# Alternating two kinds of head pairs in an attention stage, with a one-operation difference of two softmaxes

## The chip, the cores and the metric

The kernel runs on one core of a Trainium2 chip. The metric is the device time of one launch in microseconds (us), lower is better. Everything is fp32; large matmuls are made of three passes over high and low parts. The whole program is two transformer blocks in one launch. Only one stage of some 120 us of it is touched: the first mixer of the second block.

## The reference, cut to what matters

The stage mixes two kinds of attention over 256 tokens (x) and 256 context tokens (ctx). Kind A is windowed attention with a sink, 8 heads of 64 that share 2 key-value heads. Kind B is differential attention, 4 heads with two score maps each:

```
def diff_attend(q, k, v, lam):
    s = jnp.einsum('bqhmd,bkhmd->bhmqk', q, k).astype(jnp.float32) * (HEAD_DIM ** -0.5)
    p = jax.nn.softmax(s, axis=-1)
    w = p[:, :, 0] - lam * p[:, :, 1]
    return jnp.einsum('bhqk,bkhe->bqhe', w.astype(v.dtype), v)
...
    y_b = sweep_blocks(lambda q_blk, n: diff_attend(q_blk, k_all, v_all, lam), bq, Q_BLOCK)
    y_b = rms_norm(y_b, b_sub_norm) * (1.0 - lam_init)
```

Query tiles of x see all 512 keys, those of ctx only the 256 context keys.

## The kernel before

The work is cut into 32 units, called pairs because each has two score maps: 4 query tiles of 128 rows (two of x, two of ctx), and in each tile 4 units B (one differential head) and then 4 units A (two windowed heads). `Attend` writes, for each engine, what step i of a software pipeline issues; every engine executes its own list in order, and semaphores join them.

- TensorE (PE), step i: the scores of unit i (L1792); then the transposes of the probabilities of unit i-2 (L1802), 4 blocks for B, 8 for A; then the product with the values of unit i-3 (L1814). The transposes of unit i-2 wait for its probabilities **and** for `aa_copied` of unit i-3, since both use the same psum banks.
- VectorE (DVE), step i: the maxima of unit i (B: L1870; A: L1874 and two L1878, with the bias); `weights` of unit i-1 (A: the reciprocal L1886; B: L1888 to L1891); for an A unit i-2 the copy of the second turned half (L1850); the output of unit i-3 (B: L1858, A: two L1860).
- ScalarE (ACT), step i: the two exponentials of unit i (L1827), then the copy of the turned probabilities of unit i-2 (L1836).

B's `weights` waited for by PE were four operations: reciprocal of both sums, times lambda, a scaling pass over map 1 (L1890), and a pass that scales map 0 and subtracts (L1891).

Beside these steps lie side steps, one behind an Attend step at most, whose places are (j, step) in the list `side`: the norms of the last context heads (L1648, L1660, L1663) and their turns (L1727 on PE, L1737 on ACT) in the first tile; then for each finished tile t the norm of B's outputs (`SubNorm`: the Square L1975 on ACT, L1986 to L1989 on DVE, Ln and Exp L1978, L1979 on ACT, L1992 and L1995 on DVE), and two output turns (L1727 on PE, L1737 on ACT for the high part, L1747 on DVE for the low part), one for B's columns (BQ) and one for A's (AQ). The next stage, the output projection with L350 and the weight splits L292 and L298, begins when the last output turn is done.

## Time and profile before

| | us |
|---|---|
| median of 3 runs | 2790.0 (2788.89 to 2799.0) |
| the profiled execution | 2799.45 |
| its span | 2797.7 |
| PE / DVE / ACT busy in the span | 2586.2 / 1378.7 / 1021.6 |
| the stage of the change, from the first scores to the first L350 of the next stage | 1301.2 to 1422.6 |

The span is the profiled part of the execution, 1.75 us shorter than its time. The profiled execution was slower than the median by 9.45 us, about as slow as the slowest of the three runs. The stage is 121.4 us, 4.3% of the span. On every timeline row the first number is the start from the span's start and the second the duration.

### The profile page before, as it was taken

What the parts mean: (1) busy time and instruction counts of PE and PEld (TensorE: products, weight loads), DVE (VectorE), ACT (ScalarE), POOL (GpSimd) and SP (SyncE); (2) the same over time, 40 slices, a digit from 0 to 9 for tenths busy, and PEclk for the clock granted to TensorE, in tenths of its full rate; (3) what the DMA queues carried; (4) which work ended last, traced back from release to release, by engine and by line L of the source; (5) the groups of instructions that cost most, each with busy time, mean ns of one, the idle gap of its engine ahead of it and who ended that gap; (6) DMA issues with size and microseconds to landing.
All of it is one profiled execution on the core that took longest, in us unless ns stands there. A gap on an engine that the chain in (4) does not pass through costs nothing. (4 is left out here: it accounts for less than half of the span.)

```text
span 2797.7 us, 36294 instructions
## 1 busy us (share of the span) xinstructions
PE 2586.2 (92%) x15294; PEld 2167.4 (77%) x15294; DVE 1378.7 (49%) x2279; ACT 1021.6 (37%) x1603; POOL 0.2 (0%) x4
## 2 busy tenths in 40 slices
PE   7999999899989999898888999989999896858999
PEld 6888689788868888776676888868888684546998
DVE  4646554654453333468754333343333535556654
ACT  4534444443342222255523222132222242244442
POOL 0000000000000000000000000000000000000000
PEclk8999999999999999999999999999999997679999
DMA  8886733688822223253012222222222352021454
GB/s 274 280 273 192 216 126 99 206 305 311 301 83 98 98 98 98 83 165 106 1 53 76 98 98 98 98 76 98 97 94 96 98 160 66 0 76 46 159 185 139
DMA packets 145188, 372.36 MB, mean 133 GB/s; under 512 B 20202, under 2 KB 65794, under 8 KB 144898
## 3 DMA queue, kind: packets, MB, share of 16 engines
q1 hardware_dynamic: 144594, 368.21, 40.0%
q8 instruction: 122, 2.00, 0.3%
q10 hardware_dynamic: 432, 1.82, 0.2%
q14 instruction: 40, 0.33, 0.0%
HBM read 368.84 MB, written 1.15 MB: 132 GB/s over the span
## 5 line engine op out<-in xcount | busy, mean ns | idle before, releaser
L298 DVE TENSOR_TENSOR weights_lo<-weights_raw,weights_hi 128x1024 fp32r<-128x1024 f32 (+1 forms) x545 | 656.3, 1216 | 536.5 <-ACT weights_hi L292 534.1
L350 PE MATMUL psum<-normed_hi,weights_hi 128*128 128x256 f32 (+1 forms) x2560 | 863.9, 337 | 33.0 <-DVE normed_lo L549 24.3
L350 PE MATMUL psum<-normed_lo,weights_hi 128*128 128x256 f32 (+1 forms) x2560 | 847.8, 331 | 0.0
L350 PE MATMUL psum<-normed_hi,weights_lo 128*128 128x256 f32 (+1 forms) x2560 | 847.3, 331 | 0.0
L292 ACT CAST weights_hi<-weights_raw 128x1024 fp32r<-128x1024 f32 (+1 forms) x545 | 562.2, 1039 | 378.7 <-DMA weights_raw<-in_w_down 265.1
L350 PEld LDWEIGHTS psum<-normed_hi,weights_hi 128*128 128x128 f32 x2560 | 489.1, 191 | 117.6 <-issue 51.4
L350 PEld LDWEIGHTS psum<-normed_lo,weights_hi 128*128 128x128 f32 x2560 | 490.5, 192 | 44.1 <-issue 1.2
L350 PEld LDWEIGHTS psum<-normed_hi,weights_lo 128*128 128x128 f32 x2560 | 490.0, 191 | 44.0
L350 PE MATMUL psum<-hidden_lo,weights_hi 128*128 128x512 f32 x528 | 205.4, 389 | 0.0
L350 PE MATMUL psum<-hidden_hi,weights_hi 128*128 128x512 f32 x528 | 205.4, 389 | 0.0
L350 PE MATMUL psum<-hidden_hi,weights_lo 128*128 128x512 f32 x528 | 205.4, 389 | 0.0
L452 DVE SCALAR_TENSOR_TENSOR resid<-psum,mod,resid 128x256 f32<-128x256 f32 x80 | 35.8, 480 | 273.3 <-PE psum L350 273.3
L350 PE MATMUL psum<-weights_hi,normed_hi 128*128 128x512 f32 (+2 forms) x400 | 151.0, 378 | 20.7 <-DVE weights_lo L298 10.8
L588 DVE TENSOR_TENSOR arena<-arena,psum 128x512 f32<-128x512 f32 (+1 forms) x110 | 63.9, 581 | 205.9 <-PE psum L350 205.9
L580 ACT CAST hidden_hi<-arena 128x512 fp32r<-128x512 f32 x66 | 40.9, 620 | 309.3 <-DVE arena L588 309.3
L350 PE MATMUL psum<-weights_hi,normed_lo 128*128 128x512 f32 (+2 forms) x400 | 147.8, 370 | 0.0
L350 PE MATMUL psum<-weights_lo,normed_hi 128*128 128x512 f32 (+2 forms) x400 | 147.7, 369 | 0.0
L577 ACT ACTIVATE arena<-psum 128x512 f32<-128x512 f32 (+1 forms) x110 | 56.3, 512 | 247.2 <-PE psum L350 247.1
L350 PEld LDWEIGHTS psum<-hidden_hi,weights_lo 128*128 128x128 f32 x528 | 99.1, 188 | 20.7
L350 PEld LDWEIGHTS psum<-hidden_hi,weights_hi 128*128 128x128 f32 x528 | 99.1, 188 | 20.6
L350 PEld LDWEIGHTS psum<-hidden_lo,weights_hi 128*128 128x128 f32 x528 | 99.1, 188 | 20.4
L350 PEld LDWEIGHTS psum<-weights_hi,normed_hi 128*128 128x128 f32 x400 | 82.1, 205 | 37.4 <-issue 12.9
(280 smaller groups left out, 2865.6 us busy)
## 6 DMA issues: line engine op xcount, KB each, us to landing
weights_raw<-in_w_gu SPq DMA_DIRECT2D x220, 512.0 KB, 3.5
weights_raw<-in_w_down SPq DMA_DIRECT2D x110, 512.0 KB, 3.5
arena<-in_w_mod SPq DMA_DIRECT2D x72, 512.0 KB, 6.4
weights_raw<-in_w_x SPq DMA_DIRECT2D x24, 512.0 KB, 4.7
resid<-in_w_mod SPq DMA_DIRECT2D x24, 512.0 KB, 6.3
normed_raw<-in_w_mod SPq DMA_DIRECT2D x24, 512.0 KB, 6.1
under_normed_hi<-in_w_mod SPq DMA_DIRECT2D x24, 512.0 KB, 6.3
weights_raw<-in_w_qk SPq DMA_DIRECT2D x24, 512.0 KB, 3.6
```

What stands on the lines that cost most here:

```text
L292: se.copy(w_hi[:, c % RING, a], w_raw[:, c % RING, a]).then_inc(hi_ready, 1)
L298: ve.tensor_tensor(w_lo[:, c % RING, a], w_raw[:, c % RING, a], w_hi[:, c % RING, a].bitcast(F32), ALU.subtract).then_inc(lo_ready, 1)
L350: last = te.matmul(out, a, b, start=start and n == 0, stop=stop and n == 2)
L452: last = ve.scalar_tensor_tensor(out=resid[:, k, mine], in0=psum[:, self.bank(k), side * S - at0:(side + 1) * S - at0], scalar=mod[:, m, s ...
L577: se.activation(raw, self.sums(b), ACT.Silu).then_inc(evac_act, 1)
L580: se.copy(hi, raw).then_inc(hid_hi, 1)
L588: ve.tensor_tensor(raw, raw, self.sums(b), ALU.mult).then_inc(evac_dve, 1)
```

## The change

Four edits, all in this stage. (1) The units of a tile alternate B, A, B, A instead of four B and four A. (2) `weights` of a B unit: lambda is kept negated, the factor -lambda * sum0 / sum1 is made in two small operations, and one long operation (map 1 times the factor plus map 0) gives the unscaled difference; the reciprocal of sum 0 is taken after it. (3) The output of a B unit is scaled as it leaves psum, a tensor_scalar in place of a copy. (4) SubNorm gets three more small operations for very small sums, and its steps and those of the output turns move: SubNorm from behind steps 8t+8 and 8t+9 to 8t+10 and 8t+11, the first output turn is now A's, the second B's.

```diff
@@ -1854,10 +1855,7 @@
                     at0 = 0
                     for n, dest in enumerate(u.out):
                         src = psum[:, 6, at0:at0 + dest.shape[1]]
-                        if u.lam is not None:
-                            last = ve.tensor_copy(dest, src)
-                        else:
-                            last = ve.tensor_scalar(dest, src, self.stat[:, j % 4, 2 + n:3 + n], None, ALU.mult)
+                        last = ve.tensor_scalar(dest, src, self.stat[:, j % 4, 2 + n:3 + n], None, ALU.mult)
                         at0 += dest.shape[1]
                     last.then_inc(aa_out, 1)
@@ -1885,12 +1883,12 @@
                 if u.lam is None:
                     step(ve.reciprocal(stat[:, 2:4], stat[:, 2:4]))
                     return
-                step(ve.reciprocal(stat[:, 2:4], stat[:, 2:4]))
-                step(ve.tensor_tensor(stat[:, 3:4], stat[:, 3:4], u.lam, ALU.mult))
-                step(ve.tensor_scalar(s[:, 1, 0:u.width], s[:, 1, 0:u.width], stat[:, 3:4], None, ALU.mult))
-                ve.scalar_tensor_tensor(out=s[:, 0, 0:u.width], in0=s[:, 0, 0:u.width], scalar=stat[:, 2:3],
-                                        in1=s[:, 1, 0:u.width], op0=ALU.mult, op1=ALU.subtract
-                                        ).then_inc(aa_probs, 1)
+                step(ve.reciprocal(stat[:, 3:4], stat[:, 3:4]))
+                step(ve.scalar_tensor_tensor(out=stat[:, 3:4], in0=stat[:, 3:4], scalar=stat[:, 2:3], in1=u.lam,
+                                             op0=ALU.mult, op1=ALU.mult))
+                ve.scalar_tensor_tensor(out=s[:, 0, 0:u.width], in0=s[:, 1, 0:u.width], scalar=stat[:, 3:4],
+                                        in1=s[:, 0, 0:u.width], op0=ALU.mult, op1=ALU.add).then_inc(aa_probs, 1)
+                step(ve.reciprocal(stat[:, 2:3], stat[:, 2:3]))
         BK, BV, AK, AV, BQ, AQ = 0, 512, 1024, 1152, 1280, 1792
         ab = at(0, TT, 2304)
@@ -1926,7 +1924,7 @@
                 ve.tensor_reduce(lam_tmp, lam_prod, AX.X, ALU.add).then_inc(lam_dots, 1)
                 dve.wait_ge(lam_ready, 1)
                 step(ve.tensor_tensor(lam, lam_tmp[:, 0:1], lam_tmp[:, 1:2], ALU.subtract))
-                step(ve.tensor_scalar(lam, lam, 0.8 - 0.6, None, ALU.add))
+                step(ve.tensor_scalar(lam, lam, -1.0, -(0.8 - 0.6), ALU.mult, ALU.add))
         def heads_of(a, t, start, heads):
             return a[:, t, start:start + heads * HD].rearrange("p (h d) -> p h d", d=HD)
@@ -1950,12 +1948,13 @@
                                      for side in range(2)],
                                     [ab[:, t, AQ + (4 * side + h) * HD:AQ + (4 * side + h + 1) * HD]
                                      for side in range(2)], minus_sink=minus_sink[:, 2 * h:2 * h + 2]))
-            return b_units + a_units
+            return [u for two in zip(b_units, a_units) for u in two]
         sub_squares, sub_ms, sub_rstd, sub_done = (
             sem("sub_" + n) for n in ("squares_ready", "mean_ready", "rstd_ready", "normed"))
         class SubNorm(Stage):
             n = 2
@@ -1964,8 +1963,8 @@
                 self.t, self.after = t, after
                 self.base = take("sub", 1)
                 self.y = ab[:, t, BQ:BQ + 512]
-                self.r, self.fits, self.total = (small[:, 600 + 12 * self.base + 4 * k:604 + 12 * self.base + 4 * k]
-                                                 for k in range(3))
+                self.r, self.fits, self.total, self.few = (
+                    small[:, 600 + 16 * self.base + 4 * k:604 + 16 * self.base + 4 * k] for k in range(4))
             def scalar(self, act, step, i):
                 if i == 0:
@@ -1975,7 +1974,7 @@
                     se.activation(sub_sq, self.y, ACT.Square, scale=2.0 ** -20).then_inc(sub_squares, 1)
                 else:
                     act.wait_ge(sub_ms, self.base + 1)
-                    step(se.activation(self.r, self.r, ACT.Ln, scale=2.0 ** -40))
+                    step(se.activation(self.r, self.r, ACT.Ln, scale=2.0 ** 40))
                     se.activation(self.r, self.r, ACT.Exp, scale=-0.5).then_inc(sub_rstd, 1)
             def vector(self, dve, step, i):
@@ -1986,10 +1985,15 @@
                     step(ve.tensor_reduce(self.total, sub_sq.rearrange("p (h d) -> p h d", h=4), AX.X, ALU.add))
                     step(ve.tensor_scalar(self.r, self.total, 1.0 / P, EPS * 2.0 ** -40, ALU.mult, ALU.add))
                     ve.tensor_scalar(self.fits, self.total, largest, None, ALU.is_le)
-                    ve.tensor_scalar(self.r, self.r, 2.0 ** 100, None, ALU.min).then_inc(sub_ms, 1)
+                    step(ve.tensor_scalar(self.r, self.r, 2.0 ** 100, None, ALU.min))
+                    step(ve.tensor_scalar(self.few, self.r, 2.0 ** 20, None, ALU.is_le))
+                    step(ve.scalar_tensor_tensor(out=self.r, in0=self.few, scalar=2.0 ** -80, in1=self.r,
+                                                 op0=ALU.max, op1=ALU.mult))
+                    ve.scalar_tensor_tensor(out=self.fits, in0=self.few, scalar=2.0 ** -40, in1=self.fits,
+                                            op0=ALU.max, op1=ALU.mult).then_inc(sub_ms, 1)
                 else:
                     dve.wait_ge(sub_rstd, self.base + 1)
-                    step(ve.scalar_tensor_tensor(out=self.r, in0=self.r, scalar=(1.0 - (0.8 - 0.6)) * 2.0 ** -40,
+                    step(ve.scalar_tensor_tensor(out=self.r, in0=self.r, scalar=1.0 - (0.8 - 0.6),
                                                  in1=self.fits, op0=ALU.mult, op1=ALU.mult))
                     r = self.r.rearrange("p (h o) -> p h o", o=1).to_broadcast([P, 4, P])
                     ve.tensor_tensor(y, y, r, ALU.mult).then_inc(sub_done, 1)
@@ -2219,10 +2223,10 @@
         for t in range(TT):
             units += ab_pairs(t, first_needs if t == 0 else [turns.done(13)] if t == NT else [])
         attend = Attend(units, s_ab, turned_ab)
-        subs = [SubNorm(t, (aa_out, attend.base + 8 * t + 4)) for t in range(TT)]
+        subs = [SubNorm(t, (aa_out, attend.base + 8 * t + 7)) for t in range(TT)]
         out_items = []
         for t in range(TT):
-            for m in (4, 0):
+            for m in (0, 4):
                 at0 = AQ if m == 0 else BQ
                 need = (aa_out, attend.base + 8 * t + 8) if m == 0 else (sub_done, t + 1)
                 out_items.append(TurnItem([ab[:, t, at0 + j * P:at0 + (j + 1) * P] for j in range(4)], [need],
@@ -2232,7 +2236,7 @@
         o_steps = steps_of(out_turns)
         side = [(0, s) for s in h_steps[14:18]] + [(4, s) for s in t_steps[10:14]]
         for t in range(TT):
-            side += [(8 * t + 8, (subs[t], 0)), (8 * t + 9, (subs[t], 1)), (8 * t + 10, o_steps[2 * t])]
+            side += [(8 * t + 10, (subs[t], 0)), (8 * t + 11, (subs[t], 1)), (8 * t + 11, o_steps[2 * t])]
             side += [(8 * t + 12, o_steps[2 * t + 1])]
         alone(Merged(beside(steps_of(attend), side)))
         segments[-1] = (segments[-1][0], 0)
```

On VectorE the second x tile (units 8 to 15) looked like this from the maxima of B unit 9 to those of B unit 10; `L1870` are the maxima, `L1888` to `L1891` the weights of B unit 8, `L1850` and `L1860` belong to the A units of the tile before, `L1986` to `L1995` are SubNorm:

```order
L1870 TENSOR_REDUCE small<-psum 128x2
L1888 RECIPROCAL small<-small 128x2
L1889 TENSOR_TENSOR small<-small 128x1
L1890 TENSOR_SCALAR arena<-arena,small 128x512
L1891 SCALAR_TENSOR_TENSOR arena<-arena,small 128x512
L1850 COPY arena<-psum 128x512
L1860 TENSOR_SCALAR arena<-psum,small 128x64 x2
L1992 SCALAR_TENSOR_TENSOR small<-small 128x4
L1995 TENSOR_TENSOR arena<-arena,small 128x512
L1870 TENSOR_REDUCE small<-psum 128x2
```

The same place now, behind SubNorm's first half: `L1872` and `L1876` are maxima of the A unit 11, `L1886` to `L1891` the weights of the B unit 10, `L1851` and `L1858` the second copy of A unit 9 and the output of B unit 8:

```order
L1872 COPY arena<-small 128x2
L1876 ISA arena,small<-psum,const,small 128x512
L1876 ISA small 128x1
L1876 ISA arena,small<-psum,const,small 128x512
L1886 RECIPROCAL small<-small 128x1
L1887 SCALAR_TENSOR_TENSOR small<-small 128x1
L1889 SCALAR_TENSOR_TENSOR arena<-arena,small 128x512
L1891 RECIPROCAL small<-small 128x1
L1851 COPY arena<-psum 128x512
L1858 TENSOR_SCALAR arena<-psum,small 128x128
L1996 SCALAR_TENSOR_TENSOR small<-small 128x4
L1999 TENSOR_TENSOR arena<-arena,small 128x512
```

B's operations no longer follow one another: between two B weights now lie the maxima of an A unit, and SubNorm's second half (L1996, L1999) stands ahead of the maxima of unit 12 and not of unit 10.

On VectorE the stage ended so before; the last SubNorm (L1986 to L1995) stood ahead of the last unit's output (the last L1860):

```order
L1986 TENSOR_REDUCE small<-arena 128x4
L1987 TENSOR_SCALAR small<-small 128x4
L1988 TENSOR_SCALAR small<-small 128x4
L1989 TENSOR_SCALAR small<-small 128x4
L1850 COPY arena<-psum 128x256
L1860 TENSOR_SCALAR arena<-psum,small 128x64 x2
L1992 SCALAR_TENSOR_TENSOR small<-small 128x4
L1995 TENSOR_TENSOR arena<-arena,small 128x512
L1860 TENSOR_SCALAR arena<-psum,small 128x64 x2
L1747 SCALAR_TENSOR_TENSOR normed_lo<-psum,cols,normed_hi 128x4x128
L1747 SCALAR_TENSOR_TENSOR normed_lo<-psum,normed_hi 128x4x128
```

and ends so now, with the last SubNorm behind the last output and ahead of both low parts L1747:

```order
L1858 TENSOR_SCALAR arena<-psum,small 128x64 x2
L1985 TENSOR_REDUCE small<-arena 128x4
L1986 TENSOR_SCALAR small<-small 128x4
L1987 TENSOR_SCALAR small<-small 128x4
L1988 TENSOR_SCALAR small<-small 128x4
L1989 TENSOR_SCALAR small<-small 128x4
L1990 SCALAR_TENSOR_TENSOR small<-small 128x4
L1992 SCALAR_TENSOR_TENSOR small<-small 128x4
L1996 SCALAR_TENSOR_TENSOR small<-small 128x4
L1999 TENSOR_TENSOR arena<-arena,small 128x512
L1747 SCALAR_TENSOR_TENSOR normed_lo<-psum,normed_hi 128x4x128
L1747 SCALAR_TENSOR_TENSOR normed_lo<-psum,cols,normed_hi 128x4x128
```

SubNorm moved from ahead of the last output to behind it, and nothing of the stage is left beside which it could run.

## Rows read from the trace of the kernel before

**Rows 1.** Windows by tile: length, busy us (instructions) of the engines, PEclk, DMA

```profile
1301.00:1333.00 32.00, 24.02 (x128) 15.34 (x128) 25.95 (x63) 17.81 (x50) 0.00 (x0) 0.79 0.01 2
1333.00:1364.80 31.80, 26.50 (x185) 19.35 (x184) 24.88 (x67) 17.46 (x45) 0.00 (x0) 1.00 0.00 1
1364.80:1389.50 24.70, 20.50 (x147) 16.11 (x146) 18.70 (x68) 13.10 (x46) 0.00 (x0) 0.93 0.00 1
1389.50:1422.60 33.10, 23.97 (x153) 18.07 (x152) 24.10 (x87) 17.09 (x57) 0.00 (x0) 0.84 0.00 1
```

**Rows 2.** Waits of the stage: who for whom, us in total, times, longest

```profile
PEld psum L1802 <- DVE arena L1891: 22.8, 12, 3.8
```

**Rows 3.** Timeline, one A step (unit 6), from its scores to the next transposes

```profile
1325.05 0.30 PEld L1792 LDWEIGHTS psum<-arena 64*128 64x128 f32 x4 [0.17 <-issue]
...
1326.22 0.17 DVE L1874 COPY arena<-small 128x2 f32<-128x2 f32 x1 [1.14 <-PE psum L1792]
...
1327.76 0.73 ACT L1827 ACTIVATE arena<-arena,small 128x513 f32<-128x513 f32 x1 [0.98 <-DVE small L1878]
...
1329.19 0.56 ACT L1836 COPY arena<-psum 128x512 f32<-128x512 f32 x1
...
1329.82 0.86 PEld L1802 LDWEIGHTS psum<-const,arena 128*128 128x128 f32 x8 [0.81 <-ACT arena L1827]
```

**Rows 4.** Timeline, one B step (unit 11), all three engines

```profile
1347.13 0.97 PEld L1814 LDWEIGHTS psum<-arena 128*128 128x128 f32 x8
...
1347.96 1.22 DVE L1870 TENSOR_REDUCE small<-psum 128x2 f32<-128x1024 f32 x1
1348.22 0.30 PEld L1792 LDWEIGHTS psum<-arena 64*128 64x128 f32 x4
...
1349.09 0.15 DVE L1888 RECIPROCAL small<-small 128x2 f32<-128x2 f32 x1
1349.21 0.69 ACT L1827 ACTIVATE arena<-psum,small 128x512 f32<-128x512 f32 x1 [1.95 <-DVE small L1870]
...
1350.00 0.75 DVE L1891 SCALAR_TENSOR_TENSOR arena<-arena,small 128x512 f32<-128x512 f32 x1
...
1350.55 0.58 ACT L1836 COPY arena<-psum 128x512 f32<-128x512 f32 x1
1350.67 0.28 DVE L1858 COPY arena<-psum 128x128 f32<-128x128 f32 x1
1350.87 0.16 DVE L1874 COPY arena<-small 128x2 f32<-128x2 f32 x1
...
1351.20 0.42 PEld L1802 LDWEIGHTS psum<-const,arena 128*128 128x128 f32 x4 [2.68 <-DVE arena L1891]
...
1351.59 0.97 PEld L1814 LDWEIGHTS psum<-arena 128*128 128x128 f32 x8
```

**Rows 5.** Timeline, PE where it waits for nothing: scores, A transposes, A values

```profile
1336.84 0.30 PEld L1792 LDWEIGHTS psum<-arena 64*128 64x128 f32 x4
...
1337.89 0.86 PEld L1802 LDWEIGHTS psum<-const,arena 128*128 128x128 f32 x8 [0.76 <-issue]
...
1338.72 1.87 PEld L1814 LDWEIGHTS psum<-arena 128*128 128x128 f32 x16
...
1340.65 0.30 PEld L1792 LDWEIGHTS psum<-arena 64*128 64x128 f32 x4
```

**Rows 6.** Groups of the stage, shapes apart: xcount, busy us, mean ns, idle before

```profile
L1890 DVE TENSOR_SCALAR arena<-arena,small 128x512 f32<-128x512 f32 x8 | 3.9, 486 | 0.3
...
L1988 DVE TENSOR_SCALAR small<-small 128x4 f32<-128x4 f32 x4 | 0.7, 170 | 0.1
```

**Rows 7.** Timeline, the end of the stage

```profile
1417.98 0.48 DVE L1860 TENSOR_SCALAR arena<-psum,small 128x64 f32<-128x64 f32 x2 [0.47 <-PE psum L1814]
1418.43 0.69 ACT L1737 ACTIVATE normed_hi<-psum,cols 128x512 fp32r<-128x512 f32 x1 [1.94 <-PE psum L1727]
...
1420.04 1.09 PE L1727 MATMUL psum<-const,arena 128*128 128x128 f32 x4 [1.65 <-DVE normed_lo L1747]
...
1422.64 0.76 PE L350 MATMUL psum<-normed_hi,weights_hi 128*128 128x512 f32 x1 [1.50 <-DVE normed_lo L1747]
```

## The prediction

> **What bounds the kernel now.** Only one stage is touched, so I read that stage alone. First its windows by tile [rows 1]: four stretches of 32.0, 31.8, 24.7 and 33.1 us, together 121.6 us, in which PE is busy 95.0 us, VectorE 93.6 and ScalarE 65.5. No engine is full, so it is an order of work that sets the time, and the question is which wait ends last. The waits of the stage [rows 2] name VectorE's L1891, B's last operation, as the main releaser of PE's transposes: 22.8 us in 12 waits. The timeline says otherwise. In the B step [rows 4] L1891 ends at 1350.00 + 0.75 = 1350.75, ScalarE's copy L1836 of the unit before at 1350.55 + 0.58 = 1351.13, and PE starts its transposes at 1351.20. The transposes wait for both events, and the copy is the later one. In the A step [rows 3] it is the same: the copy ends at 1329.75, the transposes start at 1329.82. So there is a loop over three engines: scores of unit i, maxima of i on VectorE, exponentials of i on ScalarE, then behind them in ScalarE's list the copy of i-2, then on PE the transposes of i-1, the value product of i-2, and the scores of i+2.
>
> **The loop's prices**, for x tiles at full clock. A unit [rows 3]: scores to maxima 1.17, maxima to exponentials 1.54, those to the copy 1.43, the copy to the transposes 0.63; in sum 4.77. B unit [rows 4, 3]: maxima to exponentials 1349.21 - 1347.96 = 1.25, then 1.34 to the copy and 0.65 to the transposes; with A's 1.17 from scores to maxima 4.41. PE alone [rows 5]: scores 1.05, A's transposes 0.83, A's values up to the next scores 1.93; B's transposes 0.39, B's values up to the next scores 1.09 [rows 4].
>
> Before, the four B units of a tile followed one another. VectorE's B step is 1350.87 - 1347.96 = 2.91 us without a gap [rows 4], and the loop asks (4.41 + 0.39 + 1.09) / 2 = 2.95: both bind, and a side step on VectorE costs its full length. The four A units are bound by PE, 1.05 + 0.83 + 1.93 = 3.81 [rows 5]; the loop asks (4.77 + 0.83 + 1.93) / 2 = 3.77. One B and one A together: 2.95 + 3.81 = 6.76 us. Four of them are 27.0, and the second tile took 31.8 [rows 1]; the other 4.8 us are its side steps (SubNorm, two output turns).
>
> **What alternation makes of it.** After an odd step's scores (A) PE does A's transposes and B's values, after an even one B's transposes and A's values. PE alone needs 1.05 + 0.83 + 1.09 + 1.05 + 0.39 + 1.93 = 6.34 for both, 0.42 less than now. But the loop through an A unit is now 4.77 up to the transposes of a B unit, then 0.39, then the values of an A unit, 1.93: 7.09 us for two units. The loop through a B unit asks 4.41 + 0.83 + 1.09 = 6.33. The longer one decides: 7.09 against 6.76, **0.33 us more a pair of units**, because the slow maxima and exponentials of A now meet the slow value product of A in one round. Eight pairs in the x tiles: +2.6 us. In ctx tiles, half as wide, I take half, +1.3 us, an estimate between nothing and the same 2.6.
>
> **B's arithmetic.** Removed is the pass L1890, 0.486 us for 512 columns [rows 6], 16 of them, the ctx ones narrower: at most 7.8 us of VectorE. B's weights get ready about 0.5 us sooner. By the loop above they weren't what PE waited for, so nothing of it is on the path; it only widens VectorE's slack. Added per B unit is a second reciprocal, 0.15 [rows 4], behind the release of PE; the small scalar_tensor_tensor replaces a small product of the same kind. The output's scaling has no row at 128 columns; the nearest are the copy that it replaces, 0.28 [rows 4], and two scalings of 64 columns in 0.48 [rows 7]. It lies between the copy's 0.28 and the 0.48 of both, so 0 to 0.2 more; I take 0.06, by the copy, whose width it has. Also beside idle time. The Trainium skill, page "VectorE: DVE Perf Modes", section "The TRN2 errata", puts such a one-source pass between SBUF operands at 58 cycles plus half a cycle a column, 0.33 us for 512, an estimate; by it VectorE would be relieved of at most 5.2 us and not 7.8. No term of the sum hangs on either; the filling rival below would get less.
>
> **The side steps.** Before, they stood beside B units, where VectorE had no gap, and cost their whole length, 4.8 us a tile. Laid out by hand for the second tile, with the scores of unit 9 at 0: the pair up to the scores of 11 is the plain 7.09. SubNorm's first half comes behind step 10. It waits for the Square, which lies on ScalarE behind the copy, starts at 8.4 and takes a reduce of 0.72 and six small operations of 0.17 with their gaps [rows 6], to 10.0; the maxima of 11 wanted to start at 7.09 + 1.17 = 8.26. They are 1.75 late, on the loop. SubNorm's second half delays the maxima of 12, a B unit, which lie off the longer loop with 7.09 - 6.33 = 0.76 of slack, and the turn that follows hides the rest: nothing. The first output turn adds 0.45 on PE between a value product and the scores. Its low part on VectorE waits for its high part on ScalarE and puts the maxima of 13 off by 1.64. The second turn is hidden in the slack of the B loop. So 4 x 7.09 + 1.75 + 0.45 + 1.64 = 32.2 us, side steps 3.84, against 31.8 now: +0.4 us. SubNorm's three new operations, some 0.2 each, are in the 1.75.
>
> For the four tiles: the second +0.4. The ctx tiles, with half the loss of the loop (0.65 each) and the same 4.8 - 3.84 = 0.96 us gained on side steps, -0.3 each. In the first tile the side steps are head norms and four turns; three or four of the turns were paid by PE beside A units, two now lie in slack, one norm is paid less: +1.3 - 0.8 = +0.5, an estimate by analogy. Sum +0.3 us.
>
> **The tail.** From the last output to the first L350 it is 1422.64 - 1417.98 = 4.66 us [rows 7]; B's turn and SubNorm lay ahead of the last A output. Now the last SubNorm stands behind the last output: the reduce and six small operations 1.6, Ln and Exp with their handing over some 0.8, the scaling of 512 columns with its small one 0.9: 3.3 us. Behind it come the low part of A's turn (0.7) and the whole turn of B, which costs what the second turn costs now, 1422.64 - 1420.04 = 2.6. The first turn's 1420.04 - 1418.43 = 1.6 is hidden under SubNorm. 0.45 + 3.3 + 0.7 + 2.6 = 7.05: **+2.4 us**.
>
> **Sum:** 0.3 + 2.4 = 2.7, taken as +3 us on a profiled time of 2799.45, 0.1%. Against the median, 2790.0, I predict **2793 us**. Such a difference can't be told: a measurement of this kernel tells about 0.5%, 14 us, from no change, and its own runs lie 10 us apart.
>
> **Rivals.**
> *The stage fills up (faster).* If PE waited for L1891 after all, as the waits say [rows 2], or if the loop's handing over is shorter when VectorE has slack, the pairs go at PE's 6.34: -0.42 x 8 = -3.4 us in x, half in ctx, and the side steps vanish in VectorE's gaps, up to 3 us a tile. -5 to -16, about 2780 us. For it: 28 us of idle VectorE and 26.6 of PE [rows 1]. Against: the end of the copy stands 0.07 ahead of the transposes in both timelines.
>
> *The clock falls (slower).* The granted clock is 1.00 in the second tile, 0.79 in the first, 0.84 in the last [rows 1], where PE's turn took 1.09 [rows 7]. Alternation gives PE a wait in every round (0.75 of 7.09). If the clock sat at 1.2 GHz, PE's 6.34 a pair would be 12.7 at most, against 7.09: up to 5.6 us a pair. It decides (14 us) when as much work as 2.5 such pairs more than now runs low; with five, 2790 + 28 = 2818. Against: in the B half of the second tile PE waited longer than that, 2.68 us at once [rows 4], and kept 1.00. The Trainium skill, "TensorE: Matmul & The Clock Gate", Part 1, calls the low clock the default that activity lifts; by that rule even waits would be a risk, but the second tile's 1.00 shows them harmless so far.
>
> *The saved pass and the rest cancel (no change).* Without the loop's penalty and with the tail halved: 0 to +1, 2790.
>
> **How the numbers follow.** My own case 0.52 (-1 to +8 us); the stage fills up 0.32; nothing at all 0.12; the clock 0.04. The range is 2781 to 2803: below, the middle of the filling case; above, my case with the 10 us by which the runs of one kernel differ. It leaves out the far half of the filling case and the clock. Faster by over 0.5% needs more than 14 us, nearly all that the filling case has: 0.04. Slower by over 0.5% is the clock: 0.04. The rest 0.92.
>
> **What would show it.** Right: pairs of scores L1793 in the second tile some 7.1 us apart where no side step lies, the transposes L1803 starting 0.07 behind the end of ScalarE's copy, VectorE busy 2 to 5 us less in the stage, and 7 us from the last output to L350. Wrong: pairs at 6.4 us, transposes that start right behind B's long operation, or a stage clock below 0.7.

## The result, and the profile after the change

The changed kernel takes 2796.6 us (median of 22 runs, 2795.0 to 2811.1), the kernel before, run beside it on the same chips, 2790.5 (22 runs, 2788.2 to 2799.8). The ratio is 1.002, with a 95% interval of 1.001 to 1.0029: slower by 5.6 us (2.8 to 8.1); the two medians lie 6.1 apart. That is below the half per cent that the forecast called a difference, though the interval excludes zero. Forecast were 2793 and +3.

The profiled execution took 2795.09 us, its span is 2792.9. The windows of the four tiles of the stage, with the columns of [rows 1]:

```profile
1299.60:1332.30 32.70, 25.30 (x142) 16.70 (x142) 24.81 (x62) 16.91 (x47) 0.00 (x0) 0.79 0.00 1
1332.30:1367.10 34.80, 30.97 (x185) 22.95 (x184) 24.61 (x72) 18.07 (x46) 0.00 (x0) 0.85 0.00 1
1367.10:1392.30 25.20, 19.75 (x141) 15.46 (x140) 19.32 (x74) 13.94 (x49) 0.00 (x0) 0.93 0.00 1
1392.30:1427.60 35.30, 24.12 (x148) 18.48 (x147) 24.45 (x92) 17.04 (x57) 0.00 (x0) 0.81 0.00 1
```

From its first scores to the first L350 behind it the stage took 121.4 us before and takes 127.85 now, +6.4. So the loss is inside the stage. By tiles it is +0.8, **+3.0**, +0.5 and **+2.1**. The second tile, whose rows are shown below, stands out twice: it lost most, and its granted clock went from 1.00 [rows 1] to 0.85. VectorE's busy time in the four windows, 93.2 us, is nearly what it was (93.6), although a pass was removed.

The two profiled spans point the other way, 2797.7 before and 2792.9 now. The reason lies mostly behind the stage: from the first L350 to the end it is 1375.1 us before and 1365.4 now. Much of that comes up around 960 to 980 us behind the stage, in code that the change doesn't touch, where the granted clock was 0.50 before and 0.93 now:

```profile
2382.64:2402.64 20.00, 18.94 (x55) 10.52 (x54) 10.08 (x28) 5.02 (x12) 0.00 (x0) 0.50 0.00 0
2387.48:2407.48 20.00, 15.15 (x76) 9.00 (x75) 12.69 (x36) 7.00 (x15) 0.00 (x0) 0.93 0.00 0
```

In the thirteen profiled executions of this document the part behind the stage takes 1361 to 1375 us. So the 6.4 us are a reading of the stage alone, and how the 5.6 us of the times divide between the stage and what follows isn't shown.

The timeline of one pair of units in that tile, from the scores of one A unit to those of the next, where no side step lies (line numbers moved by one: L1793 scores, L1803 transposes, L1815 values, L1828 exponentials, L1837 ScalarE's copy):

```profile
1335.94 0.30 PEld L1793 LDWEIGHTS psum<-arena 64*128 64x128 f32 x4
...
1337.12 0.17 DVE L1872 COPY arena<-small 128x2 f32<-128x2 f32 x1 [0.52 <-PE psum L1793]
...
1338.65 0.72 ACT L1828 ACTIVATE arena<-arena,small 128x513 f32<-128x513 f32 x1 [1.86 <-DVE small L1876]
...
1338.98 0.75 DVE L1889 SCALAR_TENSOR_TENSOR arena<-arena,small 128x512 f32<-128x512 f32 x1
...
1340.08 0.56 ACT L1837 COPY arena<-psum 128x512 f32<-128x512 f32 x1
...
1340.71 0.42 PEld L1803 LDWEIGHTS psum<-const,arena 128*128 128x128 f32 x4 [1.49 <-DVE arena L1889]
...
1343.03 0.30 PEld L1793 LDWEIGHTS psum<-arena 64*128 64x128 f32 x4
```

The pair takes 1343.03 - 1335.94 = 7.09 us, and the loop from the scores to the transposes 1340.71 - 1335.94 = 4.77, both as worked out beforehand. The four parts of the 4.77 come out too: 1.18, 1.53, 1.43 and 0.63, where 1.17, 1.54, 1.43 and 0.63 were forecast. The view puts the wait of the transposes down to VectorE's L1889, but that had ended at 1339.73, nearly a microsecond earlier; ScalarE's copy ended at 1340.64, and the transposes start 0.07 behind it.

The same tile a little later, where SubNorm's first half (L1985 to L1992) stands behind step 10:

```profile
1344.44 0.69 DVE L1985 TENSOR_REDUCE small<-arena 128x4 f32<-128x512 f32 x1 [0.75 <-ACT arena L1974]
...
1346.01 1.13 PE L1793 MATMUL psum<-arena 64*128 64x512 f32 x4
1346.12 0.17 DVE L1872 COPY arena<-small 128x2 f32<-128x2 f32 x1
...
1349.09 0.56 ACT L1837 COPY arena<-psum 128x512 f32<-128x512 f32 x1
...
1349.75 1.08 PE L1803 MATMUL psum<-const,arena 128*128 128x128 f32 x4 [2.61 <-ACT arena L1837]
...
1350.63 3.51 PE L1815 MATMUL psum<-arena 128*128 128x64 f32 x16
...
1353.93 1.06 PE L1727 MATMUL psum<-const,arena 128*128 128x128 f32 x4
...
1354.92 2.08 PE L1793 MATMUL psum<-arena 64*128 64x512 f32 x4
```

SubNorm puts the maxima off by 1.9 us, they put off the exponentials and the copy, and PE waits 2.61 us at once. What PE does next goes at half speed: A's values take 3.51 us instead of 1.9, an output turn 1.06 instead of 0.6, scores 2.08 instead of 1.13. The output turn of 1359.93 takes 0.60 again. The scores of units 11 to 13 lie 11.9 us apart, where my layout had 9.3.

The end of the stage, which answers to [rows 7]:

```profile
1420.45 0.48 DVE L1858 TENSOR_SCALAR arena<-psum,small 128x64 f32<-128x64 f32 x2 [1.26 <-PE psum L1815]
1420.84 0.68 DVE L1985 TENSOR_REDUCE small<-arena 128x4 f32<-128x512 f32 x1
...
1423.30 0.69 DVE L1999 TENSOR_TENSOR arena<-arena,small 128x512 f32<-128x512 f32 x1
...
1424.74 1.09 PE L1727 MATMUL psum<-const,arena 128*128 128x128 f32 x4 [2.64 <-DVE normed_lo L1747]
...
1427.48 0.76 PE L350 MATMUL psum<-normed_hi,weights_hi 128*128 128x512 f32 x1 [1.66 <-DVE normed_lo L1747]
```

From the last output to the first L350 it is 7.03 us, against 4.66 before: SubNorm (L1985 to L1999) and a whole output turn stand behind the last unit. Up to that turn it is 4.29 us, where 4.45 was forecast, and from there 2.74, where 2.6 was.

### The profile page after: what moved, and what is told of

It is laid out like the page before. It is cut to its first block and busy times, and to the rows that moved or that the text cites. A ratio compares the mean times of both kernels' runs of the same rounds, so it can differ in the third digit from the quotient of the medians.

```text
span 2792.9 us, 36319 instructions
## 1 busy us (share of the span) xinstructions
PE 2578.5 (92%) x15294; PEld 2161.0 (77%) x15294; DVE 1378.5 (49%) x2291; ACT 1021.6 (37%) x1603; POOL 0.2 (0%) x4
## 5 line engine op out<-in xcount | busy, mean ns | idle before, releaser
L350 PE MATMUL psum<-normed_hi,weights_hi 128*128 128x256 f32 (+1 forms) x2560 | 864.0, 338 | 31.8 <-DVE normed_lo L549 23.0
L350 PE MATMUL psum<-normed_lo,weights_hi 128*128 128x256 f32 (+1 forms) x2560 | 848.0, 331 | 0.0
L350 PE MATMUL psum<-normed_hi,weights_lo 128*128 128x256 f32 (+1 forms) x2560 | 847.5, 331 | 0.0
L350 PEld LDWEIGHTS psum<-normed_hi,weights_hi 128*128 128x128 f32 x2560 | 489.2, 191 | 116.7 <-issue 51.4
L350 PEld LDWEIGHTS psum<-normed_hi,weights_lo 128*128 128x128 f32 x2560 | 489.9, 191 | 44.7
L350 PEld LDWEIGHTS psum<-normed_lo,weights_hi 128*128 128x128 f32 x2560 | 490.3, 192 | 44.0 <-issue 1.2
L350 PE MATMUL psum<-hidden_hi,weights_hi 128*128 128x512 f32 x528 | 205.4, 389 | 0.0
L350 PE MATMUL psum<-hidden_lo,weights_hi 128*128 128x512 f32 x528 | 205.4, 389 | 0.0
L350 PE MATMUL psum<-hidden_hi,weights_lo 128*128 128x512 f32 x528 | 205.4, 389 | 0.0
L350 PE MATMUL psum<-weights_hi,normed_hi 128*128 128x512 f32 (+2 forms) x400 | 149.2, 373 | 18.8 <-DVE normed_lo L549 9.9
L350 PE MATMUL psum<-weights_hi,normed_lo 128*128 128x512 f32 (+2 forms) x400 | 146.4, 366 | 0.0
L350 PE MATMUL psum<-weights_lo,normed_hi 128*128 128x512 f32 (+2 forms) x400 | 146.1, 365 | 0.0
L350 PEld LDWEIGHTS psum<-hidden_lo,weights_hi 128*128 128x128 f32 x528 | 99.1, 188 | 20.8
L350 PEld LDWEIGHTS psum<-hidden_hi,weights_lo 128*128 128x128 f32 x528 | 99.1, 188 | 20.5
L350 PEld LDWEIGHTS psum<-hidden_hi,weights_hi 128*128 128x128 f32 x528 | 99.1, 188 | 20.5
L350 PEld LDWEIGHTS psum<-weights_hi,normed_hi 128*128 128x128 f32 x400 | 79.8, 200 | 36.2 <-issue 13.7
```

The costliest lines, as they stand in the source:

```text
L350: last = te.matmul(out, a, b, start=start and n == 0, stop=stop and n == 2)
```

## The experiments

Two of them split the change, one opens the loop, three try the clock, the side steps and the tail, and five take the place of the copies further. Ratios are to the kernel before, run beside each; "stage" and "tiles" are read from the scores' starts in the profiled execution, as above. Each is one execution, so a stage is good for the mechanism and not for the last microsecond.

### The arithmetic alone

The order of before, with the new weights, the scaled output and the new SubNorm. Against the changed kernel:

```diff
-            return [u for two in zip(b_units, a_units) for u in two]
+            return b_units + a_units
-        subs = [SubNorm(t, (aa_out, attend.base + 8 * t + 7)) for t in range(TT)]
+        subs = [SubNorm(t, (aa_out, attend.base + 8 * t + 4)) for t in range(TT)]
...
-            for m in (0, 4):
+            for m in (4, 0):
...
-            side += [(8 * t + 10, (subs[t], 0)), (8 * t + 11, (subs[t], 1)), (8 * t + 11, o_steps[2 * t])]
+            side += [(8 * t + 8, (subs[t], 0)), (8 * t + 9, (subs[t], 1)), (8 * t + 10, o_steps[2 * t])]
```

> The order of the kernel before, with the one-operation difference, the scaled output and SubNorm's three new small operations. Theory L (a loop through ScalarE's copy decides, the weights of B are off the path): the B units keep their 2.95 us a unit, SubNorm's new operations (3 x 0.2 us in each of four tiles) lie beside B units and cost up to 2.4 us; in all 0 to +2 us against the kernel before. Theory F (the transposes wait for B's arithmetic, as the table of waits says): 0.5 us a B unit less on VectorE, 16 units, -4 to -8 us.

Measured: 2793.65 us, ratio 0.9998 [0.9988, 1.0009]. The arithmetic with SubNorm's new operations brings nothing that the times can tell, as the loop theory has it; a gain of 4 to 8 us is excluded. Its profile shows a stage of 125.0 us, 3.6 more than before, with tiles of 31.6, 32.1, 24.9 and 36.4: nearly all of it in the last, whose clock was 0.81 and not 0.84.

### The order alone

The alternating order, with the old weights, copy and SubNorm (the other half of the diff).

> The alternating order and the moved side steps, with the old four-operation weights, the plain copy as output and the old SubNorm. Theory L: as slow as the changed kernel, stage 127 to 129 us: 0.5 us more for the weights of B are in a slack of VectorE, the three missing operations of SubNorm give 0.6 us a tile back; +5 to +8 us against before. Theory F: slower than the changed kernel by as much as the arithmetic saves, 4 to 8 us, so +10 to +14 us against before.

Measured: 2796.38 us, ratio 1.0011 [0.9996, 1.0027], stage 124.3, tiles 33.15, 32.65, 24.2 and 34.3. Less than both theories expected. PE's B transposes in the second tile:

```profile
1340.12 0.63 PE L1803 MATMUL psum<-const,arena 128*128 128x128 f32 x4 [0.47 <-DVE arena L1851]
...
1347.41 0.63 PE L1803 MATMUL psum<-const,arena 128*128 128x128 f32 x4 [0.90 <-DVE arena L1851]
...
1356.01 0.63 PE L1803 MATMUL psum<-const,arena 128*128 128x128 f32 x4 [2.21 <-DVE arena L1851]
```

A plain pair takes 1347.41 - 1340.12 = 7.29 us, 0.2 more than with the new weights: with the old ones VectorE's list, which ends in its own copy L1851, is later than ScalarE's. In this order, then, the new arithmetic is worth 0.2 us a pair, down to the 7.09 of ScalarE's loop. PE's wait behind SubNorm, whose old form is three operations shorter, is 2.21 us; the clock stays at 1.00 in this tile, and the tile takes 32.65.

### ScalarE's copy ahead of the exponentials

If the loop runs through the copy because it stands behind the exponentials in ScalarE's list, moving it must open the loop. In the changed kernel:

```diff
 # Attend.scalar, step i
+                if 2 <= i < len(self.units) + 2:
+                    j, u = i - 2, self.units[i - 2]
...
+                    se.copy(self.turned[:, j % 2, 0, 0:w], psum[:, 4, 0:w]).then_inc(aa_copied, 1)
                 if i < len(self.units):
...
-                if 2 <= i < len(self.units) + 2:
-                    j, u = i - 2, self.units[i - 2]
...
-                    se.copy(self.turned[:, j % 2, 0, 0:w], psum[:, 4, 0:w]).then_inc(aa_copied, 1)
```

> The changed kernel with ScalarE's copy of the turned half of unit i-2 ahead of the exponentials of unit i. Theory L: the transposes no longer wait behind the exponentials; next in line is VectorE's copy of the second half, about 0.2 us earlier, so pairs of units in the x tiles go from 7.09 to about 6.9 us, -1.5 to -3 us against the changed kernel, and the late transposes that fed the low clock come earlier too. Theory F: no change, or slower because the exponentials start later.

Measured: 2788.11 us, ratio 0.9983 [0.9971, 0.9995], stage 118.8 instead of 127.85, tiles 29.9, 30.4, 23.6 and 34.9. The timeline of a pair:

```profile
1334.53 0.30 PEld L1793 LDWEIGHTS psum<-arena 64*128 64x128 f32 x4
...
1338.43 0.69 DVE L1851 COPY arena<-psum 128x512 f32<-128x512 f32 x1
...
1339.27 0.63 PE L1803 MATMUL psum<-const,arena 128*128 128x128 f32 x4 [0.63 <-DVE arena L1851]
...
1341.56 0.30 PEld L1793 LDWEIGHTS psum<-arena 64*128 64x128 f32 x4
```

The transposes now start behind VectorE's copy L1851, the other half of the same hand-over, and the pair takes 7.03. So ScalarE's copy was what PE waited for, but the plain pair gains only 0.06, because VectorE's copy is late as well. The stage gains 9 us, three times the most that I expected, and at most 0.5 of it in the eight plain pairs of x. The rest comes at side steps, with the clock that fell behind them: the second tile has 1.00 again, the third too (0.93 in the changed kernel). The price that I had put on the loop counted only the plain pairs.

### Work for PE in the long wait

If the low clock in the second tile follows from PE's standing still, giving PE something to do there must keep it. In the changed kernel, in front of the transposes of the steps that wait long; the results go to the turn bank and are never read:

```diff
+        FILL = {12: 14, 20: 16, 28: 18}
...
+                if i in FILL:
+                    pe.wait_ge(tn_done, self.turns0 + FILL[i])
+                    for _ in range(22):
+                        te.transpose(psum[:, TURN_BANK, 0:P], ident, ident)
                 pe.wait_ge(*u.probs)
```

> The changed kernel with 22 extra transposes of the identity on PE into the turn bank (their result is never read) ahead of the transposes of steps 12, 20 and 28, where PE idles 2.6, 2.4 and 2.9 us. Theory C (the 2.6 us that the second tile took over the laid out 32.2 are the low clock behind the wait of step 12): the granted clock stays at full speed in the second tile, which takes 32.2 to 33 us instead of 34.8; -2 to -4 us against the changed kernel. Rival (the low clock there comes for another reason, or the extra work delays the transposes): the second tile keeps its 34.8 us or more.

PE in the second tile (lines moved by three at the scores and by seven behind them; L1803 is the filler here), and the windows of the second and the last tile:

```profile
1348.48 1.13 PE L1796 MATMUL psum<-arena 64*128 64x512 f32 x4
1349.54 2.62 PE L1803 MATMUL psum<-const 128*128 128x128 f32 x22
1352.22 0.63 PE L1810 MATMUL psum<-const,arena 128*128 128x128 f32 x4
...
1352.69 1.90 PE L1822 MATMUL psum<-arena 128*128 128x64 f32 x16
...
1354.42 0.61 PE L1727 MATMUL psum<-const,arena 128*128 128x128 f32 x4
```

```profile
1334.70:1367.00 32.30, 28.54 (x203) 21.26 (x203) 24.81 (x72) 18.17 (x49) 0.00 (x0) 1.00 0.00 1
1392.00:1429.60 37.60, 27.55 (x170) 21.44 (x169) 24.51 (x91) 16.80 (x57) 0.00 (x0) 0.78 0.00 1
```

The clock stays at 1.00 and the instructions behind the wait have their full speed: values 1.90 instead of 3.51, turn 0.61 instead of 1.06. The transposes start 3.74 us behind the scores, against 3.75 in the changed kernel, so it was the clock that the filler changed and not the wait's end. The tile takes 32.86 us instead of 34.85, 2.0 back. So the cause of most of the second tile's loss is shown. But the last tile, with a clock of 0.78 instead of 0.81, took 2.4 us more, the stage is 127.5 us against 127.9, and the whole kernel, 2800.76 us, ratio 1.0025 [1.0009, 1.0042], gained nothing.

### Side steps beside odd steps

SubNorm and the turns of the changed kernel moved so that they delay B units' loop, which has slack:

```diff
-            side += [(8 * t + 10, (subs[t], 0)), (8 * t + 11, (subs[t], 1)), (8 * t + 11, o_steps[2 * t])]
-            side += [(8 * t + 12, o_steps[2 * t + 1])]
+            side += [(8 * t + 11, (subs[t], 0)), (8 * t + 12, (subs[t], 1)), (8 * t + 13, o_steps[2 * t])]
+            side += [(8 * t + 15, o_steps[2 * t + 1])]
```

> The changed kernel with every side step of a finished tile behind an A step or one step later: SubNorm behind 8t+11 and 8t+12, the output turns behind 8t+13 and 8t+15. Theory L: the delayed maxima are then those of a B unit, whose loop has 0.76 us of slack, so SubNorm's first half costs 1.0 and not 1.75 us and the first turn's low part 1.3 less; 1 to 2 us less in each of three tiles, -3 to -6 us against the changed kernel. Rival (the side steps cost the same wherever they stand): no change.

Measured: 2797.0 us, ratio 1.0022 [1.0007, 1.0036], stage 124.98, tiles 32.7, 32.3, 24.25 and 35.7. The profile has 2.9 us less in the stage than the changed kernel, with a shorter spell at low clock in the second tile (0.95). The times have nothing of it. A miss: 3 to 6 us were expected, and where a side step stands is not worth that in the times.

### The last tile in the old order

Only for t == TT - 1, in the changed kernel: `b_units + a_units`, SubNorm ready after unit 4, turns (4, 0) and side steps at 8, 9, 10 and 12, all as before. The tail should fall back from 7 to 4.7 us.

> The changed kernel, but the last of the four tiles keeps the order of the kernel before (four B units, then four A, SubNorm and B's turn beside them). The term of the tail says: from the last output to the next stage 4.7 us and not 7.0, -2.4 us against the changed kernel; the rest of the last tile as before. Rival: the side steps beside the last tile cost again what the tail saves, no change.

```profile
1413.00:1430.20 17.20, 11.77 (x52) 10.51 (x52) 8.77 (x34) 6.47 (x18) 0.00 (x0) 0.55 0.00 1
```

From the last output to L350 it is 5.06 us, so at least 2.0 of the tail's 2.4 us come from SubNorm and B's turn standing last; the other 0.4 stayed, in a stretch at low clock. But the last 17 us of the stage ran at a clock of 0.55. The changed kernel's last 14.5 us have 0.77:

```profile
1413.00:1427.50 14.50, 7.26 (x47) 5.42 (x45) 8.42 (x33) 6.54 (x19) 0.00 (x0) 0.77 0.01 1
```

The last tile took 37.4 us. The three tiles ahead of it, which this edit leaves alone, took 32.7, 34.9 and 25.15 with clocks of 0.79, 0.85 and 0.93, as in the changed kernel: the low clock of the second tile is no accident of one execution. Time 2795.68, ratio 1.0009 [0.9997, 1.0022]: it can't be told from the changed kernel. Inconclusive on what the tail is worth in the end.

### The copy first, in the old order

First with the new arithmetic (the first and the third experiment together):

> The order of the kernel before, B's new arithmetic, and ScalarE's copy ahead of the exponentials. Theory L: in the B halves both bounds fall together, the loop by the copy and VectorE by the removed pass, from 2.95 to about 2.6 us a unit, -3 us in x and -2 in ctx, less 2 us for SubNorm's new operations: -2 to -5 us against the kernel before. If only the alternating order profits from the early copy: 0.

Measured: 2782.53 us, ratio 0.997 [0.9956, 0.9983], stage 112.9: 8 us faster (5 to 12), and expected were 2 to 5. Then the kernel before with the moved copy as its only edit:

> The kernel before with nothing changed but ScalarE's copy ahead of the exponentials. Theory L: VectorE's 2.91 us still bind the B halves and PE the A halves; what goes is the wait behind side steps, 0 to -3 us against the kernel before. If the early copy alone is worth as much as in the alternating kernel (8 to 9 us of the stage), -5 us or more.

Measured: **2775.56 us** (2775.1 to 2783.6), ratio **0.9943** [0.9926, 0.996], 16 us faster (six runs), stage 111.4. I had expected 0 to 3 us. Its windows of the second and third tile, and a B step at the place of [rows 4]:

```profile
1332.50:1361.00 28.50, 26.53 (x185) 19.37 (x184) 24.78 (x67) 18.21 (x45) 0.00 (x0) 1.00 0.00 1
1361.00:1382.30 21.30, 19.34 (x145) 15.02 (x145) 18.46 (x68) 13.20 (x45) 0.00 (x0) 1.00 0.01 2
```

```profile
1347.12 0.30 PEld L1792 LDWEIGHTS psum<-arena 64*128 64x128 f32 x4
...
1348.64 0.68 ACT L1834 ACTIVATE arena<-psum,small 128x512 f32<-128x512 f32 x1
...
1348.76 0.75 DVE L1891 SCALAR_TENSOR_TENSOR arena<-arena,small 128x512 f32<-128x512 f32 x1
...
1349.56 0.42 PEld L1802 LDWEIGHTS psum<-const,arena 128*128 128x128 f32 x4 [2.14 <-DVE arena L1891]
...
1350.26 0.58 ACT L1826 COPY arena<-psum 128x512 f32<-128x512 f32 x1 [0.85 <-PE psum L1802]
```

Now the name L1891 is right: it ends at 1349.51 and the transposes start at 1349.56. ScalarE's copy follows the transposes instead of holding them up. In [rows 4] the same wait had the same name and was the copy's. The B step without side work on PE, from the scores of unit 11 to those of 12, goes from 2.94 us to 2.60 and an A step stays at PE's 3.82. That is 0.3 of the 3.3 us by which the second tile is shorter; 2.7 are in the two steps behind side work, 4.90 to 4.36 and 5.09 to 2.97. There a side step on VectorE no longer delays the exponentials, the copy behind them and PE in a row. The 2.60 is no steady pace: VectorE's own list in that step still takes 2.90, from 1346.72 to 1349.62.

### Three more with the copy first

The kernel before with the copy first and the new arithmetic, but the old SubNorm:

> The kernel before with ScalarE's copy ahead of the exponentials and with B's new arithmetic (one-operation difference, scaled output), but with the old SubNorm without the three new operations. Against the same order with the old arithmetic (stage 111.4 us, 2775.6): theory V (the removed pass is worth something once the copy is out of the way, because VectorE then binds the B halves) says 1 to 3 us less, stage 108.5 to 110.5. Rival (neither the pass nor the guard lies on the path): stage 111 to 112.

Measured: 2779.19 us, ratio 0.9954 [0.9936, 0.9971], stage 109.0, the shortest of all. Once VectorE's L1891 is what PE waits for, the new arithmetic is worth 2.4 us in the stage; the times don't tell this kernel from the one before it. Against the first of the two above it differs only in SubNorm, and its stage is 3.9 us shorter: 0.6 us in each of the second and third tile, the length of three operations with their gaps, and 2.7 in the last, whose clock was 0.87 and not 0.82. So in this order SubNorm's three new operations take back more of the stage than the arithmetic gives: 112.9 us with both, 111.4 with neither.

The alternating order alone, with the copy first:

> The alternating order and the moved side steps with the old arithmetic, and ScalarE's copy ahead of the exponentials. Against the same thing in the order of before (stage 111.4 us) it prices the order alone, without the loop through ScalarE: the tail's 2.4 us, and in the x pairs PE's 6.34 to VectorE's 7 us; I expect a stage of 115 to 118 us, slower than the order of before by 4 to 6 us. If the loop through ScalarE had been the only fault of alternating, the stage is under 113 us.

Measured: 2792.13 us, ratio 1.0002 [0.9989, 1.0015], stage 121.2 against 111.4 for the same edit in the old order. So alternation costs more, not less, when the loop is opened: 9.8 us in the stage, 16 in the times, where I had expected 4 to 7 in the stage. By tiles it is +1.0, +2.2, +3.3 and +3.3. A plain pair in x takes 7.30 us (2.98 + 4.32), as without the early copy, since VectorE's list is the later one; in the old order a B and an A step take 6.4 to 6.7 (2.60 to 2.90, and 3.82). Four pairs of it make 2.3 to 3.5 us for the second tile, which lost 2.2. Of the last tile's 3.3 the tail has 2.2 (6.43 us from the last output to L350, against 4.20). Where the rest lies wasn't followed; the third tile's clock was 0.93 here and 1.00 in the old order.

The changed kernel with both copies early (VectorE's L1851 moved ahead of B's weights):

```diff
 # Attend.vector, step i, behind self.maxima
-                if 1 <= i <= len(self.units):
-                    self.weights(dve, step, i - 1)
                 if 2 <= i < len(self.units) + 2:
...
                         ve.tensor_copy(self.turned[:, j % 2, 1, 0:w], psum[:, 5, 0:w]).then_inc(aa_copied2, 1)
+                if 1 <= i <= len(self.units):
+                    self.weights(dve, step, i - 1)
```

> The changed kernel with ScalarE's copy first, and on VectorE the copy of the second turned half ahead of the weights instead of behind them. Theory L: in the steps without side work the transposes of a B unit then start behind B's long operation, 4.4 us behind the scores of the A unit before and not 4.71, and the pair in the x tiles takes 6.75 us and not 7.03; -1 to -3 us against the version with the first copy early alone (2788.1, stage 118.8). If VectorE's copy was not what the transposes waited for, 7.03 stays.

```profile
1332.64 0.30 PEld L1793 LDWEIGHTS psum<-arena 64*128 64x128 f32 x4
...
1336.28 0.75 DVE L1889 SCALAR_TENSOR_TENSOR arena<-arena,small 128x512 f32<-128x512 f32 x1
...
1337.08 0.42 PEld L1803 LDWEIGHTS psum<-const,arena 128*128 128x128 f32 x4 [1.17 <-DVE arena L1889]
...
1339.54 0.30 PEld L1793 LDWEIGHTS psum<-arena 64*128 64x128 f32 x4
```

The transposes start 4.44 us behind the scores (expected 4.4), 0.05 behind L1889, and the pair takes 6.90: as laid out, nearly. Then PE waits again behind SubNorm, and the clock falls:

```profile
1345.61 1.08 PE L1803 MATMUL psum<-const,arena 128*128 128x128 f32 x4 [1.97 <-DVE arena L1889]
1346.48 3.52 PE L1815 MATMUL psum<-arena 128*128 128x64 f32 x16
```

The scores of units 12 and 13 lie 8.3 us apart, the tile has a clock of 0.89, and the gain is gone: stage 121.7, time 2792.34, ratio 0.9999 [0.9986, 1.0013]. Locally right, no gain on the whole.

## Why the prediction was right, and where it was not

**The loop: right, to the hundredth.** Forecast were 4.77 us from scores to transposes and 7.09 for a plain pair, transposes 0.07 behind ScalarE's copy; the trace shows 4.77, 7.09 and 0.07. Since the parts agree as well, this is no luck of the sum. The moved copy shows the cause: with it the transposes leave ScalarE's copy and wait for the next latest event. The rival that the stage fills up rested on the wait list's name L1891; the copy was the later of the awaited events, and the arithmetic alone brought no gain.

**B's arithmetic: off the path, right.** The arithmetic alone has a ratio of 0.9998 in the old order. In the new one it is worth 0.2 us a pair: my working had left out that VectorE's list of maxima, old weights and copy would have ended behind ScalarE's there (7.29). It did not show in the forecast, which was for both together. But VectorE was to be busy 2 to 5 us less and is 0.4 less. The removed pass L1890 was 3.9 us at 512 columns and 2.8 at 256, 6.7 in all. These groups of the changed kernel eat it:

```profile
L1858 DVE TENSOR_SCALAR arena<-psum,small 128x128 f32<-128x128 f32 x16 | 5.5, 343 | 1.4 <-PE psum L1815 1.4
L1887 DVE SCALAR_TENSOR_TENSOR small<-small 128x1 f32<-128x1 f32 x16 | 3.5, 220 | 0.6
L1891 DVE RECIPROCAL small<-small 128x1 f32<-128x1 f32 x16 | 2.5, 157 | 0.0
```

The scaling takes 0.343 where the copy took 0.286 (+0.9 us for 16; +0.06 each, as taken), the small product 0.220 where it was 0.159 (+1.0, taken as nothing), the second reciprocal 2.5, and SubNorm's three new operations of 0.16 in four tiles 2.0: 6.4 us in sum. The two widths of L1890, 0.486 and 0.353, differ by 0.133 for 256 columns. The Trainium skill's half a cycle a column ("VectorE: DVE Perf Modes", "The TRN2 errata") fits this difference, an estimate of 0.13. Its fixed 58 cycles don't fit, since the pass is 0.16 us longer than the 0.33 that the prediction took from them; the same section calls them too low and puts the fixed term at about 150 cycles as measured. That gives 0.42, an estimate, and the pass is 0.06 longer still.

**The side steps: the step that was mis-sized.** "32.2 us, side steps 3.84, against 31.8 now: +0.4 us" was the sum for the second tile; it took +3.0. The layout had each operation at full clock. SubNorm's delay leaves PE waiting 2.61 us, and the next 9 us go at half speed in part. The filler brought 2.0 of the 2.6 us back, and the order alone, without the low clock, took 32.65. The rival with the falling clock had this mechanism, at a far larger size; I had weighed it against a wait of 2.68 us that kept 1.00 [rows 4] and put nothing in the sum. That was a misreading: 2.68 is the idle time of PE's weight loads (PEld). PE itself had waited 1.88 us there, and 2.07 at the most in that tile:

```profile
1351.23 0.63 PE L1802 MATMUL psum<-const,arena 128*128 128x128 f32 x4 [1.88 <-DVE arena L1891]
```

So no trace had shown a wait of PE of 2.61 us in the second tile with the clock kept. The Trainium skill's rule ("TensorE: Matmul & The Clock Gate", Part 1) that the low clock is the default and activity lifts it speaks for this outcome; the filler agrees for this tile. The wait's length alone does not decide: behind PE's 1.97 us with both copies early the clock fell, behind 2.21 in the order alone and 2.12 with ScalarE's copy first it stayed at 1.00. The ctx tiles were given -0.3 each; the third took +0.5, the last -0.3 without its tail (+2.1 - 2.4). The first was given +0.5 and took +0.8. Neither the first nor the ctx tiles were followed in the trace, so that the first and the last came out near is not shown to be for the reasons given.

**The tail: right.** Forecast 7.05 us for the last output to L350, measured 7.03.

**The sum.** +0.3 for the tiles and +2.4 for the tail became +4.0 and +2.4 in the trace, and 5.6 in the times. The sign and the range held, the central value was half of the loss. That 2796.6 lies in the range is also owed to its width: what comes up behind the stage varies by more than the change.

**What I missed in the experiments** was larger than what I missed in the prediction. I had priced the early copy by the plain pairs, where it is worth 0.06, or 0.3 in a B step. Side steps, though, had been paid by way of exponentials, copy and PE, and the early copy takes that away: 2.7 us of the old order's second tile, whose clock is 1.00 with and without it. The stage gains 10 us; the other tiles were not followed, and in the third (0.93 to 1.00) and the last (0.84 to 0.88) the clock rose too. So the prediction's "both bind, and a side step on VectorE costs its full length" was wrong in part about its reason: where the B half turns into the A half, 2.1 us of the cost came through the copy. For alternation the plain pairs matter. In the old order the opened loop leaves a B and an A step at 6.4 to 6.7 us; alternated they take 7.03, and with VectorE's copy early 6.90.

**What stays open.** The early copy takes 16 us (11 to 21) off the time. The two profiled spans differ by 20.0: 10.0 in the stage and 10.2 behind it, where, 960 to 980 us behind the first L350, the clock was 0.50 before and 0.94 with the early copy. The profiled execution of the kernel before is one of its longest, and the shortest times of the two kernels lie 12.6 us apart. So how much of the 16 us the stage has, and whether the change in the stage moves the low clock behind it, isn't shown. Single executions and medians part by some microseconds (2784.2 and 2792.3 with both copies early). And where in the first and last tile the clock falls in a given kernel wasn't settled: the filler, the moved side steps and the last tile's old order each moved a spell instead of removing it.

The best version is the kernel before with ScalarE's copy first, 2775.6 us, which beats both kernels; with the new weights and the old SubNorm it is as fast within what the times can tell.

## What to carry to other kernels

Where an instruction waits for several events, compare the ends of all of them with its start, and don't take the name in the wait list: here the same name stood for two different causes, and the edit that followed from it was worth 16 us in the times. Compare waits on the same engine as well: the weight loads' idle time is not PE's. In an engine that works its list in order, put the short copy that the next engine's next step waits for ahead of the long operations of the following unit; what it saves is counted at the side steps too, not in the steady rounds alone. When the profiles of two kernels are compared, see first whether the difference lies in the stage that was changed. When two kinds of units are alternated, add up the loop through each kind before trusting that their busy times complement one another.

## What of the hardware I had not expected

- In the changed kernel a PE wait of 2.61 us was followed by work at half clock, in the second tile that had been at 1.00 throughout; with both copies early one of 1.97 us was too. Waits of 2.07 us before, 2.12 with ScalarE's copy first and 2.21 in the order alone kept 1.00 in that tile. 22 small transposes whose result nobody reads kept it at 1.00 here and saved 2.0 us, yet the last tile had 0.78 and lost 2.4.
- With the same matmuls in the stage, its end ran at 0.55 in one kernel (17.2 us) and at 0.77 in another (14.5 us).
- On VectorE a scalar operand that is read per partition cost 0.06 us at both widths seen: L1747, one and the same operation, takes 0.751 us with such a scale (`cols`) and 0.690 with a constant at 128 x 512, and at 128 x 1 the scalar_tensor_tensor L1887 takes 0.220 where a tensor_tensor took 0.159 in the kernel before. With a constant, L1990 at 128 x 4 takes 0.161.
